# Compression's first product turned round: 32 input columns stationary, the weights streamed into four quadrants of a bank

## The reference, cut to what matters

```python
def _compress(tok, pos_emb, w1, w2):
    B, S, hd = tok.shape
    n_cmp = (S - CMP_LEN) // CMP_STRIDE + 1          # 15
    idx = np.arange(n_cmp)[:, None] * CMP_STRIDE + np.arange(CMP_LEN)[None, :]
    blocks = tok[:, idx] + pos_emb
    hid = jax.nn.gelu(blocks.reshape(B, n_cmp, CMP_LEN * hd) @ w1)
    return hid @ w2
```

## Time and profile before

| what | value |
| --- | --- |
| device time, median of 3 runs (751.75 to 753.01) | 752.87 us |
| span of the profiled execution, first to last instruction | 750.7 us |
| PE busy in the span | 742.7 us (99%) |
| PE's weight loads busy | 733.2 us (98%) |
| DVE busy | 601.2 us (80%) |
| ACT busy | 376.9 us (50%) |
| HBM traffic over the span | 207 GB/s |

### The profile page before, as it was taken

One profiled execution on the slowest core, in us unless ns is written; L12 is line 12 of the kernel. 1 busy time (PEld: TensorE's weight loads), 2 busy tenths in 40 slices (PEclk: granted clock), 3 DMA queues, 4 the chain that ended last, 5 costly groups with the idle time before them and its releaser, 6 DMA issues.

```text
span 750.7 us, 15016 instructions
## 1 busy us (share of the span) xinstructions
PE 742.7 (99%) x6374; PEld 733.2 (98%) x6374; DVE 601.2 (80%) x897; ACT 376.9 (50%) x506; POOL 30.6 (4%) x22
## 2 busy tenths in 40 slices
PE   8999999999999999999999999999999999999998
PEld 8999999999999999999999999999999999999997
DVE  5756889889897788998998788979787886687554
ACT  6558255745676533443434547356556553434330
POOL 0000000004000000000000000201110000000000
PEclk9999999999999999999999999999999999999999
DMA  9844373342843459999987336655344565678511
GB/s 336 319 153 146 110 275 113 113 139 108 309 174 115 169 173 389 334 349 329 335 306 271 138 127 230 224 174 219 103 173 139 205 224 173 224 281 301 201 58 56
DMA packets 24113, 156.07 MB, mean 208 GB/s; under 512 B 3568, under 2 KB 3696, under 8 KB 6000
## 3 DMA queue, kind: packets, MB, share of 16 engines
q1 hardware_dynamic: 24048, 155.13, 57.6%
HBM read 154.07 MB, written 1.05 MB: 207 GB/s over the span
## 4 chain that ended last, share of the span: by engine, by line
PE 95%; DVE 2%; ACT 1%; DMA 1%; issue 1%; DVEq 0%; SPq 0%
PE bank L786 17%; PE bank L787 16%; PE bank L788 16%; PE bank L867 9%; PE bank L870 9%; PE bank L869 9%; PE bank L794 3%; PE bank L796 3%; PE bank L797 3%; PE bank L1272 2%; PE bank L1239 1%; PE bank L1249 1%; PE bank L1169 1%; DMA sb_raw<-in_stream 1%; PE bank L1322 0%
## 5 line engine op out<-in xcount | busy, mean ns | idle before, releaser
L1742 DVE TENSOR_TENSOR sb_lo<-sb_raw,sb_hi 128x2048 fp32r<-128x2048 f32 (+1 forms) x116 | 261.7, 2259 | 74.5 <-ACT sb_hi L1406 74.1
L1406 ACT CAST sb_hi<-sb_raw 128x2048 fp32r<-128x2048 f32 (+1 forms) x116 | 217.8, 1882 | 100.7 <-PE bank L870 49.3
L786 PE MATMUL bank<-sb_u_hi,sb_hi 128*128 128x256 f32 (+2 forms) x696 | 195.4, 281 | 0.0
L787 PE MATMUL bank<-sb_u_lo,sb_hi 128*128 128x256 f32 (+2 forms) x696 | 192.7, 277 | 0.0
L788 PE MATMUL bank<-sb_u_hi,sb_lo 128*128 128x256 f32 (+2 forms) x696 | 192.6, 277 | 0.0
L786 PEld LDWEIGHTS bank<-sb_u_hi,sb_hi 128*128 128x128 f32 (+2 forms) x696 | 129.6, 186 | 3.0 <-issue 2.2
L787 PEld LDWEIGHTS bank<-sb_u_lo,sb_hi 128*128 128x128 f32 (+2 forms) x696 | 129.8, 186 | 0.3
L788 PEld LDWEIGHTS bank<-sb_u_hi,sb_lo 128*128 128x128 f32 (+2 forms) x696 | 129.7, 186 | 0.2
L867 PE MATMUL bank<-sb_hid_hi,sb_hi 128*128 128x256 f32 x432 | 119.3, 276 | 0.0
L870 PE MATMUL bank<-sb_hid_hi,sb_lo 128*128 128x256 f32 x432 | 119.2, 276 | 0.0
L869 PE MATMUL bank<-sb_hid_lo,sb_hi 128*128 128x256 f32 x432 | 119.2, 276 | 0.0
(11 more groups left out here) (368 smaller groups left out, 1330.3 us busy)
## 6 DMA issues: line engine op xcount, KB each, us to landing
sb_raw<-in_stream SPq DMA_DIRECT2D x140, 1024.0 KB, 5.2
sb_raw<-in_stream SPq DMA_DIRECT2D x4, 256.0 KB, 6.6
sb_raw<-in_stream SPq DMA_DIRECT2D x2, 512.0 KB, 8.5
sb_mem_t<-in_mem SPq DMA_DIRECT2D x1, 1024.0 KB, 4.8
out<-sb_h SPq DMA_DIRECT2D x4, 256.0 KB, 2.2
sb_const<-in_constants SPq DMA_DIRECT2D x1, 830.0 KB, 10.8
sb_h<-in_x SPq DMA_DIRECT2D x1, 572.0 KB, 3.6
sb_h<-in_x SPq DMA_DIRECT2D x1, 512.0 KB, 7.0
```

The source lines that it names most:

```text
L786: nc.tensor.matmul(out, a_hi, b_hi, start=(i == 0), stop=False)
L787: nc.tensor.matmul(out, a_hi, b_lo, start=False, stop=False)
L1406: nc.scalar.copy(place(hi, s)[:, 0:n], x[:, 0:n]).then_inc(sem("hi_ready"), 1)
L1742: tt(place(lo, s)[:, 0:n], x[:, 0:n], f32(place(hi, s)[:, 0:n]), ALU.subtract) \
```

## The change

Every k keeps its product, but the operands change places: 32 columns of `cmp_in` (those of the pair of k to which it belongs) are the stationary operand, and the 128 x 128 weight block w[:, k] is moving. The result of 32 x 128 goes to the quadrant k % 4 of a bank (32 partitions each), four products adding up in each quadrant. Of a quadrant's 32 rows the 16 that belong to the other k of the pair hold nothing of use. ACT copies the 128 x 128 partial sums to `cmp_parts`, and a new step `cmp_sum` on PE multiplies them, stationary, by a 0/1 constant `pick` (128 x 16) that takes the 16 useful rows of each quadrant and adds the four up; the result is the same 128 x 16 area under the key `cmp_hidden` as before. All 16 products of an i stand now in one step between two gate blocks, and `cmp_sum` stands where part 1 stood, between the halves of the next.

```diff
-    steps([("cmp_product", 0, 0)])
-    block("gate", 3, between=[("cmp_product", 0, 1), ("cmp_hidden", 0), ("topk", 0, 0)])
-    steps([("cmp_product", 1, 0), ("topk", 0, 1), ("turn_qk", 2)])
-    block("gate", 4, between=[("cmp_product", 1, 1), ("cmp_hidden", 1), ("cmp_hid",), ("topk", 0, 2)])
+    steps([("cmp_product", 0)])
+    block("gate", 3, between=[("cmp_sum", 0), ("cmp_hidden", 0), ("topk", 0, 0)])
+    steps([("cmp_product", 1), ("topk", 0, 1), ("turn_qk", 2)])
+    block("gate", 4, between=[("cmp_sum", 1), ("cmp_hidden", 1), ("cmp_hid",), ("topk", 0, 2)])
...
+    put("pick", (i % 32 - 16 * (i // 32 % 2)) == np.arange(16)[None, :])
...
+        cmp_parts = work[:, 1792:2048].rearrange("p (i n) -> p i n", i=2)
...
-            def cmp_product(i, part):
+            def cmp_product(i):
-                key = ("cmp_hidden", i)
+                key = ("cmp_parts", i)
                 w = shaped(raw_ready(pe, ("cmp_w1", i)), ("cmp_w1", i))
-                ps = banks[lease[key][0]] if part else claim(key, "turn")
+                ps = claim(key, "turn")
                 pe.wait_ge(sem("cmp_in_ready"), i + 1)
-                x = cmp_in[:, i, :].rearrange("p (k n) -> p k n", k=16)
-                for k in half(16, part):
-                    last = nc.tensor.matmul(ps[:, 0:16], w[:, k, :], x[:, k, :], start=(k == 0), stop=(k == 15))
-                if part:
-                    fill(last, key)
+                for k in range(16):
+                    r = slice(32 * (k % 4), 32 * (k % 4) + 32)
+                    pair = 16 * (k - k % 2)
+                    last = nc.tensor.matmul(ps[r, 0:P], cmp_in[:, i, pair:pair + 32], w[:, k, :], start=(k < 4),
+                                            stop=(k >= 12), skip_group_check=True)
+                fill(last, key)
+
+            def cmp_sum(i):
+                wait_evacuated(pe, ("cmp_parts", i))
+                ps = claim(("cmp_hidden", i), "turn")
+                fill(nc.tensor.matmul(ps[:, 0:16], cmp_parts[:, i, :], cst("pick"), start=True, stop=True),
+                     ("cmp_hidden", i))
```

ACT's function for the same step, which it did not have before:

```diff
+            def cmp_product(i):
+                key = ("cmp_parts", i)
+                if i == 0:
+                    act.wait_ge(sem("rope_done"), 4)
+                ps = wait_filled(act, key)
+                free(nc.scalar.copy(cmp_parts[:, i, :], ps[:, 0:P]), key)
```

More of the change, by code:

```diff
@@ L59 @@
 CONST_WIDTHS = dict(ident=P, suffix=P, prefix=P, ones=P, causal=2 * P, strict=3 * P, cos1=64, sin1=64, nsin1=64,
-                    cos2=128, sin2=128, nsin2=128, cmpneg=2 * NC, cmp01=2 * NC, decay=RH * 2 * P)
+                    cos2=128, sin2=128, nsin2=128, cmpneg=2 * NC, cmp01=2 * NC, pick=16, decay=RH * 2 * P)
 CONST_AT = dict(zip(CONST_WIDTHS, np.cumsum([0] + list(CONST_WIDTHS.values())).tolist()))
@@ L175, in steps @@
             else:
-                if step[0] == "cmp_product" and step[2] == 0:
+                if step[0] == "cmp_product":
                     raw.append(("cmp_w1", step[1]))
@@ L583, in two_blocks_kernel @@
         rden = sb(ctx, "rden", [P, 24, 2])
-        sb(ctx, "gap", [P, P // 4])
+        sb(ctx, "gap", [P, P // 4 - 16])
         turned_hi = sb(ctx, "turned_hi", [P, 2, T], F32R)
@@ L1370, in _ @@
             run(dict(block=take, mem_v=mem_v, raw=raw_product, ssq_cols=ssq_cols, rstd_row=rstd_row, turn_qk=turn_qk, turn_tail=turn_tail, stick=stick, suffix=suffix,
-                     pv_stick=pv_stick, index=index, turn_cmp=turn_cmp, cmp_product=cmp_product, cmp_kv=cmp_kv,
+                     pv_stick=pv_stick, index=index, turn_cmp=turn_cmp, cmp_product=cmp_product, cmp_sum=cmp_sum, cmp_kv=cmp_kv,
                      cmp_scores=cmp_scores, turn_cmp_p=turn_cmp_p, cmp_pv=cmp_pv, scores=scores, turn_p=turn_p,
@@ L1660, in _ @@
                  "turn_qk": turn_qk, "turn_tail": turn_tail, "stick": stick, "suffix": suffix, "gates_c": gates_c,
-                 "cmp_hidden": cmp_hidden,
+                 "cmp_product": cmp_product, "cmp_hidden": cmp_hidden,
                  "cmp_kv": cmp_kv, "cmp_scores": cmp_scores, "turn_cmp_p": turn_cmp_p, "scores": scores,
@@ L2440, in _ @@
                     else:
-                        wait_filled(sp, ("cmp_hidden", before[1]))
+                        wait_filled(sp, ("cmp_parts", before[1]))
                 b = blocks[what[1]] if what[0] == "split" else what
```

## The result

The changed kernel takes **757.81 us** (median of 4 runs, 757.01 to 759.19) against 752.35 us for the kernel before on the same chip (4 runs, 751.75 to 753.01): ratio **1.0072**, 95% interval 1.0058 to 1.0085. Forecast was 754.9 with a range of 753.0 to 757.1. The direction was right and the size was not: +5.5 us where +2.0 was foreseen.

A forecast was written before the change was run, and what follows sets the result against it. PE was taken to bound the kernel, busy 742.7 of 750.7 us. Span 750.7 + 1.4 (wait and products) + 0.6 (clock) = 752.7; from the runs' median, 752.87 + 2.0 = 754.9 us, range 753.0 to 757.1.

The forecast's parts named there:

- The clock: Behind PE's wait, in gate 3's second half: a fall to half pace, chance a half, at most 1.8 us, 0.6 counted.
- The overlap: In the new products: four column quadrants work side by side, so an i takes T = 1.2 us, 3.8 if queued.
- The wait: At cmp_sum(0), between gate 3's halves: PE stands still 5.3 us until 94.0 for ACT's copy behind gate 2's tanh.
- The second wait: At cmp_sum(1): ACT's copy is done at 101.5, 0.2 us ahead of PE at 101.7, so the wait is hidden.
- The sum T + 0.2 = +1.4: PE's net delay after both i, without a clock fall: T + 0.2 us, +1.4 with T = 1.2.
- The delay at 102 us is the delay at the end: Sign, from gate 4's second half onward: the prediction is wrong if PE's delay there isn't the delay at the end.
- low for long: Rival, behind the wait: the clock stays low the whole half gate and more, +4.3 us, 757.2; chance 0.07.
- No stall: Rival, at cmp_sum(0): ACT has its copy done by 88.7, so PE wins 4.0 us, 748.9; chance 0.05.
- there is hardly a later wait to swallow a loss: PE's whole stream: only 2.4 us are left for other waits, so a microsecond gained or lost shows at the end.
- Paid back later: Rival, behind 100 us: a wait for DVE or ACT takes over 1 us of the delay, about 753.5; chance 0.08.

The follow-up runs named there:

- the four kernels that ran together: Changed kernel, then kept-warm kernels with tiles moved, no tile moved and only small tiles moved, on one chip: 758.03, 755.60, 753.65, 755.52 us.
- no tile moved: Changed kernel with pick in its own tile inside the former gap, so nothing else shifts: 1.0052; with 20 idle products too: 1.0020 and 1.0015.
- the two kept-warm kernels with moved tiles: Changed kernel plus 20 idle products, tiles moved as in the change: 755.60 us; with only the small tiles moved: 755.52 us.
- kept-warm kernels: Changed kernel with 20 idle fp32 products ahead of the first sum's wait, to hold the clock: 1.0040 at first timing; variants differ in tile places.
- the last tiles moved: Changed kernel plus 20 idle products, pick behind the seventh of ten small tiles, so only row scales, row sums, denominators move: 753.32 us, 1.0001.
- the copy-first kernels: Changed kernel with ACT's copy ahead of the gate's tanh and cmp_parts in a free tile: 1.0021; the same with no tile moved: 1.0000.
- the layout alone: Kernel before with constants 16 columns wider and the gap 16 narrower, products and order as before: 1.0002 and 0.9998.
- the wait alone: Kernel before, products untouched, PE waiting for gate 2's tanh ahead of part 1 of the first compression product: 760.16 us, 1.0096.
- small tiles moved: Changed kernel plus 20 idle products, pick right behind the constants, so scales, c_row, statistics, row sums, denominators move 64 bytes: 755.52 us, 1.0040.

## Why the prediction was wrong

In the four kernels that ran together the changed kernel's +5.9 us splits into three parts: +1.5 with the clock held and no tile moved, +1.9 for the tiles, +2.4 for the clock (758.03 - 755.60). They are steps of one chain, so that they add up to 5.8 tests only that the two kept-warm kernels with moved tiles agree (755.60 and 755.52). The clock and the tiles are the steps that failed.

- **The overlap**, T = 1.2 us taken: right, and a little better, 1.01.
- **The wait**, 5.3 us ending at 94.0, released by ACT's copy behind gate 2's tanh: right, 4.97 us ending at 93.6. The copy took 0.25 where 0.3 was taken.
- **The second wait** hidden by 0.2 us: right, 0.1 with the clock held; in the changed kernel it is 1.5, because the low clock made PE still later than the copy.
- **The sum T + 0.2 = +1.4**: right. With the measured T it is +1.2; the six profiles of kept-warm kernels have +1.1 at gate 4's middle, and two timings with no tile moved +1.5 us. "The delay at 102 us is the delay at the end" held where no tile moved. The third timing that bears on it, with the last tiles moved, has 0.0 against a kernel before that was slow on its chip.
- **The clock is the term that was mis-sized.** The prediction gave the fall a chance of a half and took 0.6 us. It fell in every execution of the changed kernel and cost 1.8, 2.1 and 2.4 us in three pairs of medians, at or above the upper end that the prediction gave, 1.8. Two things were misread. 4.9 us behind the last matmul the clock had fallen: in the profile after, with 5.0 us of wait, it fell at 93.5, at the very end; but in the three later profiles of this change it had fallen before 92, some 3 us into the wait. One instance at the kernel's end was taken for the time that a fall needs. And the low stretch is 3.4 or 6.8 us, while the start of the kernel had shown only the shorter. (The windows at the start give 1.00 as the granted clock, so that the half pace there is the clock's was inferred; the profile after bears it out, with starts 0.21 us apart at 0.50, near the 3.51 / 16 = 0.22 at the start.) The rival "low for long" was priced at +4.3 and given 0.07; with 6.8 us low and no tile moved the trace shows +3.0 and the timing +3.5.
- **The 16 columns in the constants had no term at all.** They were named among the edits and priced at nothing without a row behind it. With the new products they cost 1.9 us by the timing on one chip, and every trace with the tiles moved shows some of it. Without this term even the measured clock would have given 754.9 - 0.6 + 2.4 = 756.7, 1.1 us short.
- **"No stall", -4.0 us**, rested on "there is hardly a later wait to swallow a loss". For a loss that holds, for a gain it doesn't: the copy-first kernels won 3.7 to 4.0 us by 103 us and had lost them by 119, since DVE had only one gap of 1.2 us in that stretch, in a wait for ACT, and its order was unchanged. The rival's price should have been near 0, which is what the better of the two showed (1.0000).
- **"Paid back later"** did not happen in the changed kernel.

What stays open: why the place of tiles that the products of the weight blocks don't read sets the pace of some stretches, which of the first four tiles it is, and why the layout alone loses 0.7 and 1.6 us in its traces and nothing in its timings. Those fell on the two chips on which the kernel before was slowest (753.9 and 753.4 us against 752.0 to 752.8), and the layout alone was never timed on one of the others.

## What to carry to other kernels

Price a wait of PE by its length plus what the clock takes behind it: here 5.0 us of standing still cost 5 us and about 2 more, and 20 idle products in the wait gave these 2 back. Before a saving on PE is counted, ask in both directions: a full PE passes every loss on to the end, but it passes a gain on only as far as the next engine that is as full as itself, here DVE in the next 20 us. And when a constant is added, put it where no other tile moves: at 0.2% the shift weighs as much as the change. Timing the shift by itself didn't find it here; comparing the starts of the same instruction in two traces did.

## What the runs showed of the hardware that had not been expected

**Column quadrants overlap completely, if issued in turn.** 16 fp32 products of 128 moving columns on four quadrants of columns took 1.01 us, against an estimated 16 x 0.22 = 3.5 us one behind the other, a factor of 3.5. Quadrant by quadrant they took about 2.4. The Trainium skill (TensorE: Matmul & The Clock Gate, Measured speedup vs the span model) gives 2.38x for three column tiles and 3.07x for four row tiles, both with 512 moving columns; this trace is above both, for four column tiles with 128.

**The low stretch of the clock came in three lengths.** It was 3.4 us in the profile after, 6.8 us in three other profiles of this change, and 10.2 us where products of 16 moving columns followed the wait (the wait alone, one profile).

**DVE and POOL hold each other up at 176 to 180 us,** and which of them waits turns on about 0.1 us. In the kept-warm kernel with no tile moved, then with small tiles moved:

```profile
177.59 2.32 DVE L1764 TENSOR_TENSOR sb_lo<-sb_raw,sb_hi 128x2048 fp32r<-128x2048 f32 x1
...
176.46 4.61 POOL L1713 TENSOR_TENSOR sb_qk_t<-sb_qk_t,sb_masked 128x512 f32<-128x512 f32 x2 [148.59 <-DVE sb_masked L2244]
```

```profile
179.47 3.35 DVE L1764 TENSOR_TENSOR sb_lo<-sb_raw,sb_hi 128x2048 fp32r<-128x2048 f32 x1
...
178.13 2.54 POOL L1713 TENSOR_TENSOR sb_qk_t<-sb_qk_t,sb_masked 128x512 f32<-128x512 f32 x2 [149.42 <-DVE sb_masked L2244]
```

Either DVE's residue takes 2.32 us and POOL's two additions 4.61, or 3.35 and 2.54. The Trainium skill (SBUF — State Buffer, Who interferes with whom) has DVE and GpSimd share one pair of ports, which one of them locks, and says that the order of issue decides who is blocked. The trace agrees: in the first form the residue starts 0.12 us ahead of POOL's second addition (177.59 against 177.71), in the second 0.09 us behind it (179.47 against 179.38), and the later one loses, 2.1 us on the one side or 1.0 on the other. All eight profiles with the small tiles in place (or only the last ones moved) have the first form, nine of the ten with them moved the second, the layout alone among these, and it goes with the first of the two places above. PE falls back 0.8 to 0.9 us between 163 and 186 us in these nine and in no other; in six of them it has won back 0.6 to 0.7 of it by 217 us, so this is not the whole of the 1.9 us.
